# Two transformer blocks with a routed mixture: seats of the experts, results put back through ones and zeros, and products computed across

## The reference

```
hybrid layer:  proj = rms_norm(x) @ w_in;   q, k of the mLSTM part = silu(depthwise_conv(proj[:, :1024]))
               x = x + concat(y_m, y_a) @ w_out
               u = relu(rms_norm(x) @ w_up);  x = x + (u * u) @ w_down          # width 4096, not gated
second block:  layer 0: x = layer_norm(a x + pool(x));  x = layer_norm(a x + swiglu(x))
               layer 1: x = layer_norm(a x + nsa(x))                            # norm "l2" in the kernel
               logits = x @ router;  top 2 of 8 experts, shares = softmax of the two
               y = sum over e of share_e * ((silu(x w_g) * (x w_u)) @ w_down_e) # width 3584
               x = layer_norm(a x + y)                                          # norm "l3"
```

## Time and profile before

| what | value |
|---|---|
| runs | 2259.03, 2263.12, 2268.36 us |
| the profiled execution | 2262.86 us, span 2261.0 us |
| TensorE / weight loads | 2140.9 / 1723.4 us busy |
| VectorE / ScalarE | 1601.9 / 1319.2 us busy |
| mean granted clock of TensorE | 0.973 of full speed |
| read from HBM | 521.5 MB, 231 GB/s over the span |
| chain that ended last | PE 68%, DVE 19%, issue 5%, ACT 5%, DMA 3% |

### The profile page before, as it was taken

The page is one execution under the profiler, slowest core; times in us unless marked ns, Lnnn a source line. Parts: engine busy times, 40 slices in busy tenths (PEclk is TensorE's granted clock), DMA queues, the critical chain, the costliest instruction groups (busy, mean ns, idle before and its releaser), DMA issues.

```text
span 2261.0 us, 26000 instructions
## 1 busy us (share of the span) xinstructions
PE 2140.9 (95%) x10012; PEld 1723.4 (76%) x10012; DVE 1601.9 (71%) x1566; ACT 1319.2 (58%) x1378; POOL 20.4 (1%) x32
## 2 busy tenths in 40 slices
PE   8889999989999999999888999999999999999997
PEld 7767887767888788877667888788888877777775
DVE  5866555776555645566756555788888899999998
ACT  6454444644544443444544544576776788888876
POOL 0000000000000000000000000000000000000000
PEclk9999999999999999997899999999999999999999
DMA  6314443422654345442007554789898999999995
GB/s 265 140 47 172 187 186 132 177 94 75 251 186 185 141 182 191 159 144 75 1 19 280 205 218 180 271 343 350 331 372 331 365 361 421 390 421 377 421 383 247
DMA packets 74625, 524.29 MB, mean 232 GB/s; under 512 B 8736, under 2 KB 9184, under 8 KB 12160
## 3 DMA queue, kind: packets, MB, share of 16 engines
q1 hardware_dynamic: 71712, 511.64, 58.5%
q0 software_dynamic: 2784, 10.93, 1.4%
HBM read 521.48 MB, written 1.05 MB: 231 GB/s over the span
## 4 chain that ended last, share of the span: by engine, by line
PE 68%; DVE 19%; issue 5%; ACT 5%; DMA 3%; DVEq 0%; SPq 0%; ACTq 0%
PE psum L518 58%; DVE LO L509 10%; DMA ring<-in_experts 2%; ACT HI L501 2%; DVE AR L1585 1%; PE psum L1055 1%; PE psum L2460 1%; PE psum L904 1%; PE psum L1050 1%; PE psum L841 1%; PE psum L686 1%; PE psum L667 1%; PE psum L1977 1%; PE psum L2523 1%; DVE AR L858 1%
## 5 line engine op out<-in xcount | busy, mean ns | idle before, releaser
L509 DVE TENSOR_TENSOR LO<-ring,HI 128x2048 fp32r<-128x2048 f32 x379 | 850.5, 2258 | 391.1 <-ACT HI L501 388.9
L501 ACT ACTIVATE HI<-ring 128x2048 fp32r<-128x2048 f32 x379 | 712.7, 1887 | 350.7 <-PE psum L518 339.5
L518 PE MATMUL psum<-HI,XT 128*128 128x512 f32 (+1 forms) x3152 | 803.9, 393 | 20.1 <-issue 5.1
L518 PEld LDWEIGHTS psum<-HI,XT 128*128 128x128 f32 x3152 | 592.0, 191 | 162.6 <-DVE XT L702 10.6
L518 PE MATMUL psum<-LO,XT 128*128 128x512 f32 (+1 forms) x1856 | 507.5, 395 | 17.1 <-DVE LO L509 14.6
L518 PEld LDWEIGHTS psum<-LO,XT 128*128 128x128 f32 x1856 | 345.6, 190 | 112.7 <-DVE LO L509 44.5
L518 PE MATMUL psum<-HI,HTH 128*128 128x512 f32 x848 | 305.4, 401 | 6.8 <-DVE HTH L1107 6.8
L509 DVE TENSOR_TENSOR LO<-AR,HI 128x2048 fp32r<-128x2048 f32 x112 | 254.7, 2289 | 53.5 <-ACT HI L501 52.9
L501 ACT ACTIVATE HI<-AR 128x2048 fp32r<-128x2048 f32 x112 | 212.5, 1910 | 59.0 <-PE psum L518 57.1
L518 PE MATMUL psum<-LO,HTH 128*128 128x512 f32 x848 | 229.1, 392 | 0.0
L518 PE MATMUL psum<-HI,HTL 128*128 128x512 f32 x568 | 221.5, 390 | 0.0
(11 more groups left out here) (281 smaller groups left out, 1462.8 us busy)
## 6 DMA issues: line engine op xcount, KB each, us to landing
ring<-in_experts SPq DMA_DIRECT2D x224, 1024.0 KB, 6.7
ring<-in_dense SPq DMA_DIRECT2D x149, 1024.0 KB, 4.8
AR<-in_experts SPq DMA_DIRECT2D x112, 1024.0 KB, 6.9
bcs<-in_ln_g POOLq DMA_DIRECT2D x4, 512.0 KB, 4.5
bcs<-in_ln_b POOLq DMA_DIRECT2D x4, 512.0 KB, 5.1
bcs<-in_norm_g POOLq DMA_DIRECT2D x3, 512.0 KB, 3.9
cons<-in_cons POOLq DMA_DIRECT2D x1, 1317.0 KB, 8.0
X<-in_x SPq DMA_DIRECT2D x2, 512.0 KB, 3.9
```

The costliest lines, as they stand in the source:

```text
L501: e.activation(HI[:, h:h + m], slot(u), ACT.Copy).then_inc(*high.up(u))
L509: e.tensor_tensor(LO[:, h:h + m], slot(u), HI[:, h:h + m].bitcast(F32), ALU.subtract).then_inc(*low.up(u))
L518: ins = e.matmul(out_ap, lhsT=a, rhs=b, start=start and n == 0, stop=stop and n == len(pairs) - 1)
```

## The change

The experts' order becomes rank 0, 4, 1, 5, 2, 6, 3, 7 (`SEATS`) in `PERM`, in the thresholds and in `KINDS`, so on side 1 the seats have 128 + 64, 64, 128, 64, 128, 64, 128, 64 slots. For an expert of one `P` tile on side 1 (seats 2, 4, 6) the result is put back as a high part (ScalarE) and a low part (VectorE, new) in `HTH` and `HTL`, through a list of ones and zeros in a free part of `XT`, as fast float32 products; the other experts keep the plain product. No list is multiplied by the share: the add takes it as a scalar. In chunks 1 to 7 of `ff0` and `ff1`, and for the second half of q and k, `across` computes features x tokens directly: 128 columns of weights are stationary and all 256 tokens stream; the transposes and, for q and k, a round of copies go. In the norms `l2` and `l3` the pieces of the two tiles are put in another order.

```diff
+SEATS = [0, 4, 1, 5, 2, 6, 3, 7]
+        def across(e, use, key, x_ready):
...
+            for i, u in enumerate(us):
+                hv, lv = hi_lo(u)
+                last = i == len(us) - 1
...
+                e.wait_ge(*high.of(u))
+                for b in range(2):
+                    for j in range(2):
+                        products(e, banks.get(*use, b)[:, j * S:j * S + S],
+                                 [(hv[:, k, tile(b * 2 + j)], z[:, i * n + k, :]) for k in range(n)
+                                  for z in (XTH, XTL)], i == 0 and j == 0, False)
+                e.wait_ge(*low.of(u))
+                for b in range(2):
+                    for j in range(2):
+                        ins = products(e, banks.get(*use, b)[:, j * S:j * S + S],
+                                       [(lv[:, k, tile(b * 2 + j)], XTH[:, i * n + k, :])
+                                        for k in range(n)], False, last and j == 1)
...
+        def still(c, gated):
+
+            return c >= 1 and not gated
+
         def net_up_tensor(e, use, key, c, kinds, gated, ready, swap, tile1=None):
+            if still(c, gated):
+                return across(e, (use, "up", c), (key, "up", c), ready)
...
         def net_turn_tensor(e, use, c, n, kinds, gated):
             hb = c % 2
+            if still(c, gated):
+                return
...
             hb, nb = c % 2, n // P
+            if still(c, gated):
+                for b in range(2):
+                    xh = HTH[:, hb, 2 * b:2 * b + 2, :]
+                    e.wait_ge(*a_done.of(use, "turn", c, b))
+                    e.wait_ge(*v_order.last)
+                    e.tensor_tensor(HTL[:, hb, 2 * b:2 * b + 2, :],
+                                    GS[:, hb, b, :].rearrange("p (j s) -> p j s", j=2),
+                                    xh.bitcast(F32), ALU.subtract).then_inc(
+                        *v_done.up(use, "turn", c, b))
+                return between()
...
-            cols(e, ("raw", l, 1), ("qk", l, 1), BOTH, xr)
+            across(e, ("raw", l, 1), ("qk", l, 1), xr)
             few(e, ("gates", l), ("gates", l), xr)
-            pad_tensor(e, l, 0)
+            pad_tensor(e, l)
             cols(e, ("mv", l), ("mv", l), BOTH, xr,
                  mid={0: lambda: few_turn(e, ("gates", l), ("gates", l))})
-            pad_tensor(e, l, 1)
...
-            for t in range(2):
-                evict(e, ("raw", l, 1), t, raw[1][:, t, :])
+            pad_across(e, l)
...
+        KINDS = [[kinds[r] for r in SEATS] for kinds in KINDS]
+        WIDTH = [[sum(kind) for kind in kinds] for kinds in KINDS]
+
+        def parted(x, side):
+
+            return (side == 1 or x == LAST - 1) and KINDS[side][x] == (P,)
...
+        def result_parts(nh):
+
+            return HTH[:, nh, :, P:S], HTL[:, nh, :, P:S]
...
                     bank = banks.take(e, "scatter", x, st, side, nh, t)
-                    e.wait_ge(*a_bank.of("ye", x, st, side, nh))
-                    e.matmul(bank, lhsT=PB[:, x % 2, st, tile(t)], rhs=YE[:, st, half(nh)], start=True,
-                             stop=True).then_inc(*filled.up("scatter", x, st, side, nh, t))
+                    if parted(x, side):
+                        for i, y in enumerate(result_parts(nh)):
+                            e.wait_ge(*(v_bank if i else a_done).of("ye", x, st, side, nh))
+                            ins = e.matmul(bank.rearrange("p (j s) -> p j s", j=4),
+                                           lhsT=places(x, side, 1)[:, t, :], rhs=y, start=i == 0,
+                                           stop=i == 1)
+                    else:
+                        e.wait_ge(*a_bank.of("ye", x, st, side, nh))
+                        ins = e.matmul(bank, lhsT=PB[:, x % 2, st, tile(t)], rhs=YE[:, st, half(nh)],
+                                       start=True, stop=True)
+                    ins.then_inc(*filled.up("scatter", x, st, side, nh, t))
...
+        def result_lo(e, x, side):
+            for nh in range(2):
+                hi, lo = result_parts(nh)
+                e.wait_ge(*a_done.of("ye", x, 0, side, nh))
+                e.wait_ge(*v_order.last)
+                e.tensor_tensor(lo, psum[:, pair(x)[nh], :].rearrange("p (j s) -> p j s", j=4),
+                                hi.bitcast(F32), ALU.subtract).then_inc(
+                    *v_bank.up("ye", x, 0, side, nh))
 
         def scatter_vector(e, x, st, side, split=False):
 
+            if parted(x, side):
+                result_lo(e, x, side)
...
-                    e.tensor_tensor(y, y, banks.get(*use), ALU.add).then_inc(*v_bank.up(*use))
+                    e.scalar_tensor_tensor(y, banks.get(*use), SHARE[:, t, x:x + 1], y, ALU.mult,
+                                           ALU.add).then_inc(*v_bank.up(*use))
...
-                weights_vector(e, x, side)
+                else:
+                    slots_vector(e, x, side)
                 if x < LAST:
                     slots_vector(e, x + 1, side)
...
                     residual_projected(e, ("po", 2), "l2", t, nh, ALPHA)
-                ln_apply(e, "l2", t, *vector("l2"), *vector("l2b"))
-                if t == 0:
+                ln_mean(e, "l2", t)
+                ln_center(e, t, *vector("l2"))
+                if t:
                     cols_lo(e, "l2", 0)
+                ln_sum(e, "l2", t)
+                ln_rows(e, "l2", t, *vector("l2b"))
...
-                ln_apply(e, "l3", t, *vector("l3"), *vector("l3b"))
+                ln_mean(e, "l3", t)
+                if t:
+                    ln_sum(e, "l3", 0)
+                ln_center(e, t, *vector("l3"))
+            for t in range(2):
+                if t == 0:
+                    ln_sum(e, "l3", 1)
+                ln_rows(e, "l3", t, *vector("l3b"))
```

More of the change, by code:

```diff
@@ L1010, in net_up_scalar @@
                 if c >= 2:
-                    e.wait_ge(*filled.of(use, "turn", c - 2, len(kinds) - 1))
+                    if still(c - 2, gated):
+                        e.wait_ge(*v_done.of(use, "turn", c - 2, t))
+                    else:
+                        e.wait_ge(*filled.of(use, "turn", c - 2, len(kinds) - 1))
                 e.wait_ge(*a_order.last)
@@ L1056, in net_turn_tensor, with net_turn_scalar @@
                 ins.then_inc(*filled.up(use, "turn", c, t))
-        def net_turn_scalar(e, use, c, n, kinds, between):
+        def net_turn_scalar(e, use, c, n, kinds, between, gated=True):
             hb, nb = c % 2, n // P
+            if still(c, gated):
+                for b in range(2):
+                    e.wait_ge(*v_done.of(use, "gate", c, b))
+                    if c >= 2:
+                        e.wait_ge(*filled.of(use, "downed", c - 2))
+                    e.wait_ge(*a_order.last)
+                    e.activation(HTH[:, hb, 2 * b:2 * b + 2, :],
+                                 GS[:, hb, b, :].rearrange("p (j s) -> p j s", j=2),
+                                 ACT.Copy).then_inc(*a_done.up(use, "turn", c, b))
+                return between()
             for t, kind in enumerate(kinds):
@@ L1108, in net_turn_vector, with net_down_tensor @@
                                 ALU.subtract).then_inc(*v_done.up(use, "low", c, t))
-        def net_down_tensor(e, use, key, c, last, acc, kinds):
-            ready = [(v_bank if kind == P else v_done).of(use, "turn" if kind == P else "low", c, t)
-                     for t, kind in enumerate(kinds)]
+        def net_down_tensor(e, use, key, c, last, acc, kinds, gated):
+            ready = [(v_done if still(c, gated) or kind != P else v_bank).of(
+                use, "turn" if kind == P else "low", c, t) for t, kind in enumerate(kinds)]
             n = 0
@@ L1269, in build, with pad_tensor @@
         ML_OUT = [BA[i] for i in (2, 0, 1, 0)]
-        def pad_tensor(e, l, part):
+        def pad_tensor(e, l):
             for t in range(2):
-                bank = banks.take(e, "pad", l, part, t)
-                e.wait_ge(*a_bank.of("raw", l, part, t))
+                bank = banks.take(e, "pad", l, 0, t)
+                e.wait_ge(*a_bank.of("raw", l, 0, t))
                 for j in range(4):
-                    ins = e.transpose(bank[:, tile(j)], raw[part][:, t, tile(j)], ident)
-                ins.then_inc(*filled.up("pad", l, part, t))
+                    ins = e.transpose(bank[:, tile(j)], raw[:, t, tile(j)], ident)
+                ins.then_inc(*filled.up("pad", l, 0, t))
         def sums_tensor(e, l):
```

148 lines of the change are left out of this document (102 added, 46 removed).

## The result

The changed kernel takes 2278.05 us (median of 7 runs) against 2263.12: 1.0068 times, 95% interval 1.0049 to 1.0087. I had said 2255 with a range up to 2267. One of the seven runs took 4042.74 us at a granted clock of 0.919; it is not in the ratio, and nothing is read from it. The profiled execution is the fastest of the runs, 2271.94 us with a span of 2270.0, so the two profiles differ by 9 us and the medians by 15.

A forecast was written before the change was run, and what follows sets the result against it. TensorE was taken to bound 128-slot experts, VectorE 64-slot ones. Experts 2.8, ungated networks 3.6, q and k -1.3, norms 1.7 and 0.9 sum to 7.7 us gained: 2262.9 to 2255.2, said 2255, range 2242 to 2267.

The forecast's parts named there:

- The turns: Expert order: three more 64-slot experts stand behind a TensorE-bound one, 2.8 us saved each, 8.4 us gained.
- clock stretch: 64-slot experts: 3.4 us at granted clock 0.50 after TensorE idled, priced 1.7 us; two charged, 3.4 us.
- The low part: Seams behind three 128-slot experts: TensorE idles about 3 us for VectorE's subtractions; 0.95 us lost each, 2.85 us.
- Rival 3: 64-slot experts behind a 128-slot one: wait for VectorE's subtractions absorbed nowhere, 8 us each, 2273 us; chance 0.08.
- Rival 2: Expert order: each 128-slot expert behind a 64-slot one gives back 2.8 us, no gain, 2263.6 us; chance 0.24.
- Ungated networks: 14 chunks in two layers: eight transposes out, 96 products of 256 columns for 48: 0.26 us a chunk, 3.6 us gained.
- Rival 4: 256-column products exposed to weight loads at 0.19 us each, 6.7 us more a pass, 16 passes, 2362 us; chance 0.03.
- q and k across: Second half of q and k, two layers: TensorE's gates turn 0.63 us later, 1.3 us lost in both.
- Norms: Layer norms: tile 1's rows 1.7 us sooner before the router, 0.9 us gained at the end.
- The signs: Wrong if 128-slot expert behind 64-slot exceeds 128 us, 64-slot falls under 106, or 256-column products stand over 0.125 us apart.

## Why the prediction was wrong, point by point

- **The step that failed** is one that the sum doesn't have. I charged the new constants and the smaller `par` at nothing, without a word, and took every row of an untouched instruction over as it stood. `XT`, `HTH` and `HTL` went off the multiple of 64 bytes, and 3609 products of 512 columns with a contiguous stationary operand (1681 from `XT` and 1032 from `HTH` and `HTL` ahead of the experts, 896 in the first and the 128-slot ones) went from 0.2267 to 0.2333 us: 3609 x 0.0066 = 23.8 us at most, of which the 16 passes across, 0.24 us shorter at that place, give back up to 3.8. The runs show 20.2 by the medians (2278.05, and 2257.89 with the places restored) and 22 by the ratios. Without it the kernel is at 0.9970 of before: 6.8 us gained, where I had 7.7 (by the two profiled executions 2.2).
- That agreement is partly luck. **The turns** were to gain 8.4 us. They gained 0.6 and 2.6 by the spans of the two pairs of kernels and 4.5 and 5.4 by the medians; the intervals tell neither pair apart. I had read 110.8 - 108.0 = 2.8 us as the worth of a neighbour. 1.7 of it was the clock stretch that the later K experts had and the first had not, and I counted it as saved by the place; in the old order with the share in the add, a K behind a P has it too and takes 109.4. About 1 us more came off a K behind a K, from 110.8 to 109.8; I put it down to the share's multiplications, which no run took alone. What that one execution leaves for the neighbour is 0.4 us. That VectorE (102 of 110 us) and the transfers (DMA share 0.97 to 0.99) hold a K whatever stands before it is my reading and is not tested.
- **The low part.** The wait was right, 3.00 us at each of three seams. Its price was not: 0.95 us and a share of the clock stretches, 6.25 in all, against 8.5 and 8.9 in the experts. I let the idle time be absorbed by VectorE's queue, but the clock falls behind it (0.75 in the 4 us from 1680 on), and the K does not win that back. Rival 3 had this mechanism, at 8 us a seam; the seams cost about 3.
- **Rival 2** did not happen: at restored places a P behind a K took 126.96 to 127.07 us, a P behind a P 126.97 and 127.26 (both read with the plain product as well).
- **Ungated networks:** 0.26 us a chunk foreseen, 0.25 measured at the places on which the earlier trace rows stand. In the kernel after, 0.21: the pass gained 0.49 and the products from `HTH` lost 0.28. Rival 4 is refuted at 0.114 to 0.121 us a product in every placing. That the size was right is partly luck: in the earlier trace rows `XT` is the stationary operand and the weights stream, in a pass across it is the other way round, and I took the one's price for the other. The form of the earlier trace rows itself took 11.51 us in the kernel before and after (806.66 to 818.17).
- **q and k across:** the gates' turn came at 46.49 instead of 45.53 us, 1.0 us later where I had 0.63; the second layer I did not read apart.
- **Norms.** In front of the router, from the residual of tile 0 to the rows of tile 1, 1170.11 to 1180.99 is 10.88 us against 12.45: 1.57, foreseen 1.7. From that residual to the experts' first product the kernel before took 37.36 us and the kernel after 34.62, so this stage gained 2.7 us; what beside the norm did it, no run parts. At the end 2256.28 to 2266.00 is 9.72 against 10.40: 0.68, foreseen 0.9. Order of time, VectorE, kernel after, answering to the earlier trace rows:

```profile
1180.99 1.54 DVE L851 SCALAR_TENSOR_TENSOR X<-AR,SML,bcs 128x512 f32<-128x512 f32 x2
```

```profile
2256.28 0.75 DVE L2953 SCALAR_TENSOR_TENSOR X<-psum,AR 128x512 f32<-128x512 f32 x1 [3.30 <-PE psum L2690]
...
2266.00 1.54 DVE L851 SCALAR_TENSOR_TENSOR X<-AR,SML,bcs 128x512 f32<-128x512 f32 x2
```

- **The signs** were set only on what the change touches. One on an untouched product ("0.227 us in the third network") would have found it at a glance.

## What to carry to other kernels

An edit to the table of tensors is an edit to every instruction behind it: work out where each operand of the commonest product begins before and after, and keep the multiple that it had. When a kernel comes out slower than its parts, compare first the pace of instructions that nobody touched. A profile is one execution: see where its time lies among the runs before a difference of a few us is read from it. A short stage that looks cheaper than its neighbours is read with its clock before its saving is given to what stands ahead of it, and a wait of 3 us on TensorE cost clock behind it at all three seams here, which ran at 1.00 without the wait.

## What the runs showed of the hardware

- A fast float32 product of 512 columns repeats after 0.2267 us with stationary and moving operand at multiples of 128 bytes, 0.2288 with the stationary one at 64 beyond, 0.2333 (0.232 with both) with either at 32 beyond a multiple of 64, and 0.2333 with a stationary operand in steps of two elements. The Trainium skill, "SBUF — State Buffer", section "Operand start alignment", asks for a multiple of the element size and says that this is about what is legal, not about speed; all these places are legal by it, and the runs show that they differ by 3%.
- Products of 256 columns with `XT` moving took mostly 0.1185 us with it at 32 bytes beyond a multiple of 64, 0.114 to 0.119 at 64 beyond one of 128, 0.121 at a multiple of 128, by the length of the pass over 96: another order than for 512 columns, and not fixed by that place alone. Not explained.
- TensorE idle for 1.06 us and, after one product, for 3.0 us at a seam was followed by a granted clock of 0.75 from 1680 to 1684 us, of 0.69 from 1916 to 1920 and of 0.51 from 2155 to 2160, at the three seams of the kernel after. With the plain product the three seams ran at 1.00.
- The same kernel differs from run to run by up to 24 us (the kernel before 2252.8 to 2277.1 in 29 runs), with the mean granted clock (0.977 in the fastest of these runs, 0.967 in the slowest). That is why differences of 5 us are read here from stretches of the traces beside the medians; where the two disagree, as on the turns, the size stays open.
